# Forming the modulation vectors of a kernel's prologue on two engines, with its panels reordered and late constants

## The reference, cut to what matters

```python
for l in range(DEPTH):
    ada = jax.nn.silu(c) @ w_ada[l] + b_ada[l]                 # c [1, 1024], w_ada[l] [1024, 6144]
    sh_m, sc_m, g_m, sh_f, sc_f, g_f = jnp.split(ada[:, None, :], 6, axis=-1)
    h = rms_norm(x, norm_mix[l]) * (1.0 + sc_m) + sh_m         # x [1, 256, 1024]
    (q_a, kc_a, vc_a, ks_a, ...) = jnp.split(h @ w_in[l], split_at, axis=-1)
    ...
```

## Time and profile before

| | us |
|---|---|
| median of 3 runs | 2214.38 (2214.07 to 2215.04) |
| the profiled execution | 2202.08 |
| its span | 2200.3 |
| TensorE busy in the span | 2052.1 (93%) |
| VectorE busy | 1482.0 (67%) |
| ScalarE busy | 1096.7 (50%) |
| GpSimd busy | 25.0 (1%) |

### The profile page before, as it was taken

The page is one execution under the profiler, slowest core; times in us unless marked ns, Lnnn a source line. Parts: engine busy times, 40 slices in busy tenths (PEclk is TensorE's granted clock), DMA queues, the critical chain, the costliest instruction groups (busy, mean ns, idle before and its releaser), DMA issues. The chain is left out here.

```text
span 2200.3 us, 32166 instructions
## 1 busy us (share of the span) xinstructions
PE 2052.1 (93%) x12896; PEld 1830.2 (83%) x12896; DVE 1482.0 (67%) x2412; ACT 1096.7 (50%) x1738; POOL 25.0 (1%) x46
## 2 busy tenths in 40 slices
PE   3899899999899899999998889899999997889999
PEld 2779888888789888898896668788898897788888
DVE  6677678877685586567757475577667757645774
ACT  2545445544545355445545554455455545545552
POOL 0101000000000000000000000000000000000000
PEclk7999999999999999999999989999999998799999
DMA  8535448876354376556555224256555553232554
GB/s 296 161 134 200 171 135 280 269 266 197 133 192 142 127 225 197 182 182 189 178 189 173 96 77 134 89 179 191 178 182 181 178 166 115 77 115 91 181 184 139
DMA packets 266068, 372.42 MB, mean 169 GB/s; under 512 B 8384, under 2 KB 160192, under 8 KB 265920
## 3 DMA queue, kind: packets, MB, share of 16 engines
q1 hardware_dynamic: 264224, 367.48, 51.4%
q10 hardware_dynamic: 1696, 2.89, 0.4%
HBM read 369.28 MB, written 1.05 MB: 168 GB/s over the span
## 5 line engine op out<-in xcount | busy, mean ns | idle before, releaser
L2081 DVE TENSOR_TENSOR parts<-ring,parts 128x2048 fp32r<-128x2048 f32 (+3 forms) x308 | 680.3, 2210 | 449.8 <-ACT parts L663 449.4
L663 ACT ACTIVATE parts<-ring 128x2048 fp32r<-128x2048 f32 (+3 forms) x308 | 569.5, 1849 | 630.6 <-PE psum L1377 328.5
L1377 PE MATMUL psum<-h,parts 128*128 128x512 f32 x1920 | 676.4, 397 | 0.0
L1375 PE MATMUL psum<-h,parts 128*128 128x256 f32 x1920 | 539.7, 281 | 2.4 <-DVE parts L2081 2.4
L1377 PEld LDWEIGHTS psum<-h,parts 128*128 128x128 f32 x1920 | 360.5, 188 | 87.2
L1375 PEld LDWEIGHTS psum<-h,parts 128*128 128x128 f32 x1920 | 362.7, 189 | 3.1 <-DVE parts L2081 3.0
L1369 PE MATMUL psum<-h,parts 128*128 128x256 f32 (+1 forms) x2088 | 269.3, 289 | 10.8 <-DVE h L2081 4.7
L1369 PEld LDWEIGHTS psum<-h,parts 128*128 128x128 f32 (+1 forms) x2088 | 259.0, 194 | 13.8 <-issue 12.2
L1369 PE MATMUL psum<-parts,h 128*128 128x512 f32 (+1 forms) x864 | 216.1, 405 | 13.2 <-DVE parts L2081 12.0
L1369 PEld LDWEIGHTS psum<-parts,h 128*128 128x128 f32 x864 | 164.7, 201 | 49.0 <-issue 8.1
L1369 PE MATMUL psum<-hid_hl,parts 128*128 128x256 f32 x1584 | 189.9, 282 | 0.9 <-DVE parts L2081 0.9
(11 more groups left out here) (241 smaller groups left out, 2201.5 us busy)
## 6 DMA issues: line engine op xcount, KB each, us to landing
ring<-in_w_ada SPq DMA_DIRECT2D x48, 1024.0 KB, 5.5
ring<-in_w_ffn_in SPq DMA_DIRECT2D x88, 512.0 KB, 4.9
ring<-in_ffn_w_gate SPq DMA_DIRECT2D x88, 512.0 KB, 4.0
ring<-in_ffn_w_up SPq DMA_DIRECT2D x88, 512.0 KB, 5.0
ring<-in_w_in SPq DMA_DIRECT2D x36, 1024.0 KB, 5.0
ring<-in_ffn_w_down SPq DMA_DIRECT2D x32, 1024.0 KB, 5.1
ring<-in_w_ffn_out SPq DMA_DIRECT2D x16, 1024.0 KB, 5.1
ring<-in_ffn_w_down SPq DMA_DIRECT2D x16, 768.0 KB, 4.4
```

The source lines that it names most:

```text
L663: act.activation(out, in_, func, **kw).then_inc(*sig(name, *keys))
L1375: pe.matmul(bank[:, 0:S], wt_hl[1], act[:, 0, :], start=start, stop=False, skip_group_check=True)
L1377: return pe.matmul(bank.rearrange("p (a s) -> p a s", a=2), wt_hl[0], act, start=False, stop=stop, skip_group_check=True)
L2081: dve.tensor_tensor(out, a, b, op).then_inc(*sig(name, *keys))
```

## The change

1. The order of the first panels. Before: groups 0, 1, 2, 3 (two panels each), then win 1 panel 0, win 1 panel 1. After: group 2, group 0, win 1 panel 0, group 1, group 3, win 1 panel 1.
2. Groups 0 and 1 (shift) are made on TensorE (`row_of`): eight fp32 products with one column of `scol` as the stationary operand and 512 weight columns moving, summed in one PSUM row; ScalarE copies the row to SBUF (`row_copy`); four products with a single 1 turn it into four columns. Group 2 and 3 stay on VectorE.
3. The norm of layer 0 is in two parts: chunks 0 to 3 after groups 2 and 0, chunks 4 to 7 after groups 3 and 1. TensorE runs both rows ahead of the first product, and group 3's column sums after three of its eight chunks.
4. `angles` runs at VectorE's start, sine and table load on ScalarE after the squares of `x`.
5. `cols` is loaded ahead of `x`. Only 416 columns of `const` are loaded at the start; rows, the other constants, `pe` and `w2` are issued by SP behind the last panel of the first product.

```diff
-ADA_FIRST = 4
+ADA_FIRST = (2, 0, 1, 3)
+N_FIRST = 416        # const: ident, ones, tri, inv come first
...
-    for i in range(ADA_FIRST):
-        ada(0, i)
+    for i in ADA_FIRST:
+        for n in range(2):
+            src = rows(w["w_ada"][0])[:, 4 * n:4 * n + 4, 512 * i:512 * i + 512]
+            out.append((("ada", 0, i, n), "first", [(0, src)]))
+    late = out[4:]
+    del out[4:]
     for l in range(L):
         win = w["w_in"][l]
         for i in ORDER:
             group(("win", l), i, win, EDGES[i], EDGES[i + 1])
+            out[-1:-1] = late
+            late = []
...
+        ada_row = {i: tok[0:1, 512 * i:512 * i + 512] for i in range(2)}
...
@@ sync
-            for name, dst, src in (("x", x[:], w["x"].rearrange("(c p) t -> p c t", p=P)),
-                                   ("cols", cols[:], w["cols"])):
+            for name, dst, src in (("cols", cols[:], w["cols"]),
+                                   ("x", x[:], w["x"].rearrange("(c p) t -> p c t", p=P))):
...
+                if key == (("win", 0), ORDER[0], 1):
+                    for name, dst, src in (
+                            ("rows", rowsb[:], w["rows"].broadcast_to([P, N_ROW])),
+                            ("masks", const[:, N_FIRST:N_CONST], w["const"][:, N_FIRST:N_CONST]),
+                            ("pe", pe_t[:], w["pe_t"]), ("w2", w2[:], w["w2"])):
+                        sp.dma_start(dst, src).then_inc(
+                            *sig(f"load_{name}", f"loaded {name}", by=16))
...
@@ scalar
-                    if c == 3 and meanwhile is not None:
+                    if c == (3 if prior else chunks - 1):
                         meanwhile()
...
                 stats(st, x, squares, DC, D, lambda c: x_ready(st, c), prior,
-                      (lambda: splits.until((first, g, 0))) if prior else None)
+                      (lambda: splits.until((first, g, 0))) if prior else trigs)
+                if prior is None:
+                    splits.until((first, g, 0))
+                    row_copy(0)
+                    normed_hi(st, range(4), h, shift)
+                    row_copy(1)
                 splits.until((first, g, 1))
-                normed_hi(st, DC, h, shift)
+                normed_hi(st, range(DC) if prior else range(4, DC), h, shift)
...
+            def trigs():
+                act.wait_ge(*at("angles"))
+                run(trig[:], turn[:, 0:2], ACT.Sin, "act_trig", "trig")
+                act.preload_act_table_set(EXP_LN)
+
+            def row_copy(i):
+                job = ("ada row", 0, i)
+                act.wait_ge(*at(("full", job)))
+                run(ada_row[i], psum[0:1, tally.bank(job), :], ACT.Copy, "act_copied",
+                    ("copied", job), ("free", job))
...
@@ tensor
+            def row_of(i):
+                key = ("ada row", 0, i)
+                b = open_bank(key, (BANKS + i,))
+                for half in range(2):
+                    panel = ("ada", 0, i, half)
+                    v = raw(panel, 4, 512)
+                    pe.wait_ge(*at("silu c"))
+                    pe.wait_ge(*at(("panel", panel)))
+                    for c in range(4):
+                        n = 4 * half + c
+                        mm = pe.matmul(b[0:1, :], scol[:, n:n + 1], v[:, c, :], start=n == 0,
+                                       stop=n == DC - 1)
+                    mm.then_inc(*sig("pe_ada", ("released", panel),
+                                     *([("full", key)] if half else [])))
+                pe.wait_ge(*at(("copied", key)))
+                b = open_bank(("ada", 0, i), (BANKS + i,))
+                for j in range(4):
+                    mm = pe.matmul(b[:, j:j + 1], ada_row[i][:, P * j:P * j + P], ones[0:1, 0:1],
+                                   start=True, stop=True)
+                mm.then_inc(*sig("pe_ada", ("full", ("ada", 0, i))))
...
-                    for i in range(ADA_FIRST):
-                        ada_cols(0, i, (BANKS + i,))
+                    ada_cols(0, 2, (BANKS + 2,))
+                    for i in range(2):
+                        row_of(i)
...
-                whole_of(win(1))
+                steps = win(1)
+                if l == 0:
+                    advance(steps, 3)
+                    ada_cols(0, 3, (BANKS + 3,))
+                whole_of(steps)
...
@@ vector
                 refine(rstd[:], newton[:, 0, :], newton[:, 1, :])
+                if vectors is not None:
+                    vectors(0)
...
                 for c in range(chunks + 1):
+                    apart = vectors is not None and c == 4
                     if c:
                         settle()
+                    if apart:
+                        low(3)
+                        vectors(1)
...
+            angles()
             dve.wait_ge(*at("silu c"))
-            for i in range(ADA_FIRST):
-                ...
+            for n in range(2):
+                ada_add(("ada", 0, 2, n))
...
+                def vectors(n):
+                    first = (("win", 0), ORDER[0], n)
+                    if n:
+                        for half in range(2):
+                            ada_add(("ada", 0, 3, half))
+                        ada_take(0, 1)
+                        ada_take(0, 3)
+                    else:
+                        ada_take(0, 2)
+                        ada_take(0, 0)
+                    adaptive(0, 8, "norm_mix", 4 * n, 4 * n + 4)
+                    splits.until(first)
```

More of the change, by code:

```diff
@@ L161, in wide @@
             group(name, g, a, c, min(c + width, a.shape[1]), deep)
-    def ada(l, i):
-        for n in range(2):
-            out.append((("ada", l, i, n), "ada",
-                        [(0, rows(w["w_ada"][l])[:, 4 * n:4 * n + 4, 512 * i:512 * i + 512])]))
     def between(first, stage, every):
@@ L419, in ada_acc @@
         def ada_acc(l, i):
-            if l == 0 and i < ADA_FIRST:
+            if l == 0 and i in ADA_FIRST:
                 return sq[:, i % 2, :]
@@ L426, in ada_acc @@
             return area[:, 512 * (g % 2):512 * (g % 2) + 512]
+        ada_row = {i: tok[0:1, 512 * i:512 * i + 512] for i in range(2)}
         def ada_before(l, i):
+            if l == 0 and i in ADA_FIRST:
+                return None
             stage, g = next((st, groups.index((l, i))) for st, groups in ADA_GROUPS.items()
@@ L683, in _, with stats @@
             splits = Splits(split)
-            def stats(st, src, dst, chunks, width, ready, prior, meanwhile=None):
+            def stats(st, src, dst, chunks, width, ready, prior, meanwhile):
                 for c in range(chunks):
@@ L700, in normed_hi @@
             def normed_hi(st, chunks, dst, shift):
-                for c in range(chunks):
+                for c in chunks:
                     act.wait_ge(*at(("piece", st, c)))
@@ L2142, in ada_add, with norm @@
                         stt(acc, v[:, k, :], c, acc, ALU.mult, ALU.add, "dve_ada", *keys)
-            splits = Splits(split, ada_add, 2 * ADA_FIRST)
-            def norm(st, chunks, gain, dst, src, shift, first, g=0):
+            splits = Splits(split, ada_add)
+            def norm(st, chunks, gain, dst, src, shift, first, g=0, vectors=None):
                 dve.wait_ge(*at(("ln", st)))
@@ L2155, in norm, with low @@
                 refine(rstd[:], newton[:, 0, :], newton[:, 1, :])
+                if vectors is not None:
+                    vectors(0)
+                def low(i):
+                    keys = [("h", st, i)] + [("h", st, "last")] * (i == chunks - 1)
+                    dve.wait_ge(*at(("h hi", st, i)))
+                    stt(dst[:, 1, i, :], piece[:, i % 4, :], shift(i),
+                        dst[:, 0, i, :].bitcast(F32), ALU.add, ALU.subtract, "dve_normed", *keys)
                 for c in range(chunks + 1):
+                    apart = vectors is not None and c == 4
                     if c:
                         settle()
+                    if apart:
+                        low(3)
+                        vectors(1)
                     if c < chunks:
@@ L2162, in norm @@
                             ALU.mult, "dve_piece", ("piece", st, c))
-                    if c >= 1:
-                        i = c - 1
-                        keys = [("h", st, i)] + [("h", st, "last")] * (i == chunks - 1)
-                        dve.wait_ge(*at(("h hi", st, i)))
-                        stt(dst[:, 1, i, :], piece[:, i % 4, :], shift(i),
-                            dst[:, 0, i, :].bitcast(F32), ALU.add, ALU.subtract, "dve_normed",
-                            *keys)
-                        if i == 2:
-                            splits.until((first, g, 1))
+                    if c >= 1 and not apart:
+                        low(c - 1)
+                    if c == 3 and vectors is None:
+                        splits.until((first, g, 1))
             def ada_take(l, i):
```

54 lines of the change are left out of this document (14 added, 40 removed).

## The result

The changed kernel takes 2201.1 us, median of 6 executions (2195.05 to 2202.8), where the kernel before took 2214.23 beside it (6 executions, 2207.24 to 2215.86): 0.994 of the time, 95% interval 0.9922 to 0.9959, 13.1 us less. The prediction was 2205.0, 9.4 us less. The sign and the chain of the start came out; the size did not, and the median lies just outside the range, on the fast side.

A forecast was written before the change was run, and what follows sets the result against it. TensorE was taken as the bound from 64.9 us on; its second product starting at 55.0, 9.9 us sooner, less 0.5 downstream, gave 9.4 us: 2214.38 - 9.4 = 2205.0 us, range 2202.0 to 2212.5.

The forecast's parts named there:

- Transfers: Program start: fewer bytes ahead of the first panel, 4.2 us less; x at 7.3 us, panels at 10.1, 12.9, 15.7.
- Angles: Program start: VectorE's 3.6 us and ScalarE's 2.9 us go into idle time, cost nothing, and remove the hole.
- An instruction of a row: Shift rows on TensorE: 0.50 us each taken, between 0.43 and 0.59; first four of row 0 at 0.9.
- the 9.9: Restart of TensorE: second large product starts at 55.0 us, not 64.9, so 9.9 us sooner.
- Rival 2: Start: gain handed back through panel slots; one late landing or slow row leaves 4.5 us, both leave nothing; chance 0.20.
- Downstream: From 64.9 us on: TensorE is the bound, so most of the 9.9 us stays; 0.5 us taken off.
- The third rival: Start: clock stays low through both rows, product ends at 71.0, 6 us later than 64.9; 2220.4 us; chance 0.10.
- Rival 1: Start: rows cost little and the chain is shorter; gain 11 to 13 us, 2202.4 us; chance 0.10.
- Rival 4: Start: sine ends after the sums of squares, so 1/rms is late; given no chance.

The follow-up runs named there:

- consts_early: Changed kernel with all constants loaded at the start again, on ScalarE's queue; 7.3 us less than the kernel before (ratio 0.9943 to 0.9975).
- again_after: The changed kernel measured once more, without an edit; 14.7 us less than the kernel before (ratio 0.9904 to 0.9952).
- angles_late: Changed kernel with angles, sine and table load put back behind the first norm; ratio 0.9993 to the kernel before.
- before_gap: Kernel before with 30 zero products in TensorE's wait ahead of layer 0's key transposes, sums started anew, losing part of one; ratio 0.9984.
- delay9: Changed kernel with nine idle VectorE instructions (4.91 us) ahead of chunk 4 of h; 5.1 us less than the kernel before (ratio 0.9965 to 0.9997).
- before_fill: Kernel before with 30 zero products, added to running sums, in TensorE's wait ahead of layer 0's key transposes; 6.8 us less (ratio 0.9955 to 0.9987).
- after_fill: Changed kernel with 30 zero products, added to running sums, ahead of layer 0's key transposes; ratio 0.9959 to the kernel before.
- best_fill: Changed kernel with zero products in two early TensorE waits and ahead of the key transposes, late constants one panel later; 2191.66 us against 2211.47 before.
- late_fill: Changed kernel with late angles and 30 zero products, added to running sums, ahead of layer 0's key transposes; ratio 0.9962 to the kernel before.
- warm_both: Changed kernel with zero products on TensorE ahead of row 0 (14) and chunk 4 (30); 14.0 us less than the kernel before (ratio 0.9910 to 0.9957).

## Where the prediction was right, and the step that failed

**The start, step by step.** Transfers: x landed for squares at 7.15 (7.3 predicted), group 2 from 9.93 to 16 (10.1 to 16.1). Angles: between 5.9 and 9.5 us on VectorE, the sine at 9.62, no stall: free, as taken. An instruction of a row takes 0.43 us at the high clock (7.06 / 16 is 0.44), the lower bound; 0.50 was taken. At the low clock it is 0.85, but for seven or eight instructions and not four: row 0 took 9.95 us (9.6), row 1 7.06 (8.0). The misses nearly cancelled: the first product started at 37.94 (38.1).

The transfers of the changed kernel, as in the earlier trace rows:

```profile
x<-in_x SPq DMA_DIRECT2D x1, 1024.0 KB, 6.0
...
rowsb<-in_rows SPq DMA_DIRECT2D x1, 736.0 KB, 8.8
...
const<-in_const SPq DMA_DIRECT2D x1, 708.0 KB, 10.0
```

x takes 6.0 us instead of 10.8, as most of the constants no longer stand beside it (8.1 with them back, in consts_early); the constants take longer at their new place than at the old one.

**Where it lost 2 us of the 9.9.** The second w_in panel, issued at 36.25, took 7.4 us to land and not 5.0 to 5.5, beside 1.6 MB of late constants: its high half began at 43.66, the low one at 45.68 (44.6 predicted). Then GpSimd, released at 45.51 by the landed rows, works while VectorE makes h: 0.77 us an instruction where the earlier trace rows have 0.48. I had put the tables down as harmless since they are not on the path; they were, beside it. Chunk 4 came at 50.25 (48.4) and TensorE's wait was 4.52 us (2.7). The high half of the next panel, at 52.75, stands right behind chunk 7 of h on ScalarE: 56.97 us and not 55.0. The clock fell once more behind the wait and made the first product some 1 us longer, beside this chain. Rival 2 had named this direction (the slots and the constants slipping a late panel), with a price of 4.5 us; the second panel's high half slipped by 1.7 (42.0 expected). One sum of the prediction is off by 0.5 us: the next panel, with its slot free at 39.4 and 5.0 and 4.5 us to come, would land at 48.9 and not at 49.4. It changed nothing, as the high half was not expected before 50.8; the panel took 10.5 us and landed at 50.4.

**The step that failed: "Downstream".** "What comes after should move with that point", less 0.5 us: the term was -0.5 and measured +5 to +6 (13.1 - 7.8 = 5.3, 14.7 - 8.7 = 6.0). I took the time behind the first products as a fixed length that moves as a block. It is not fixed, because the clock in it is not. I had read the earlier trace rows to 102 us only, where the clock is 0.98 on average, and looked at how busy TensorE was, not at how its waits and the clock behind them would change.

The traces say this only in part. Take the sooner start from each gain of the table; what is left came about behind the start. Of the eighteen traces, the kernel before among them, nine have a clock of 0.96 or more from 65 to 300 us, and in them 5.6 us are left on average (2.7 to 10.4); in the nine with 0.95 or less 1.2 us (-3.8 to 5.8). By the wait alone the parting is poorer: the nine with 2.7 us have -0.2 to 6.1, the other three with 3.8 us -3.8, -2.1 and 3.3.

The mean clock of every execution, which was taken along with its time, says it more fully. One minus this clock, times the span, is what TensorE lost to the low clock in that execution (an upper estimate, as it counts the idle time in these stretches too). From it goes the part that falls ahead of the first low half, by the traces 15.4 us in the kernel before and 3.4 in again_after.

| run | clock, mean of its executions | beside it, before | lost less behind the start, us | gain of the mean beyond the start, us |
|---|---|---|---|---|
| again_after | 0.9648 | 0.9575 | 4.8 | 6.3 |
| angles_late | 0.9610 | 0.9575 | -4.2 | -2.6 |
| before_gap | 0.9595 | 0.9578 | 3.9 | 3.5 |
| delay9 | 0.9609 | 0.9573 | -1.4 | -1.7 |
| before_fill | 0.9603 | 0.9571 | 7.4 | 6.0 |
| after_fill | 0.9629 | 0.9571 | 2.0 | 0.3 |
| best_fill | 0.9663 | 0.9571 | 7.3 | 8.6 |

Worked out for all sixteen repeats and experiments, each with the part ahead of the low half from its own trace, the two last columns differ by 1.8 us at most, and their correlation is 0.93. So what the kernels gain or lose beyond the start is what the clock gives or takes there; for the changed kernel this is some 5 of the 6 us. That the clock can be moved without touching the start, and takes the time along, is shown by before_fill, and less surely by late_fill, whose interval (0.9945 to 0.998) barely meets that of angles_late (0.9976 to 1.0009).

**The third rival.** The rows did bring the clock back to its high level after 6 us and held it through row 1. The Trainium skill, "TensorE: Matmul & The Clock Gate", section "HAM oscillation — how this bites in real kernels", tells of short bursts of thin products between waits that all run at the low clock: the trace bears it out for the first half of row 0, at 0.51, and not for the rest, as row 1 ran at 1.00.

**The other rivals.** Rival 1 (11 to 13 us, 2202.4) has nearly the right time for the wrong reason: its 0.43 us held, its restart at 51.8 did not. Even warm_both, with both rows at the high clock, restarts at 54.16:

```profile
54.16 5.69 PE L1391 MATMUL psum<-parts,h 128*128 128x512 f32 x24 [1.14 <-DVE parts L2134]
```

That the measured median lies 1.3 us from this rival's is luck. Rival 4 fell at once: the sine ended at 9.97, four microseconds ahead of the sums of squares. The chances given to a smaller gain and to rival 3 (0.30 together) went to sizes of the start, and none to a larger effect behind it; that is why the range ended at 2202.0.

**What stays open.** Why the low stretches fall where they do. warm_both has the long wait and a clock of 0.98, delay9 the short one and 0.94, and delays ahead of chunk 4 cost more at the end than they take. These runs show that the placing depends on what stands ahead of it and differs between executions of one kernel; they give no rule by which to forecast it, nor do they say why the changed kernel's clock is the better one. How the whole gain divides among the parts of the change is not shown to the microsecond either, as the intervals of the single kernels overlap.

## What to carry to other kernels

A shift at the start of a long kernel is not passed on one to one when TensorE's clock moves behind it: read the granted clock over the whole stretch that is to be shifted, and give the range a term for it in both directions, here some 5 us. One trace is one execution: compare the mean clocks of all executions, not those of two traces. A wait of TensorE there, filled with products of zeros added to a running sum, is a cheap trial (6.8 us in the kernel before, nothing in the changed one, on intervals of some 4 us to either side). "Late" constants share the queues with the panel that is critical at that moment, and what they release, here GpSimd's tables, runs beside VectorE's critical instructions.

## What was not expected of the hardware

- An fp32 product with one column as the stationary operand and 512 moving columns takes 0.43 us an instruction (two to a product) at the high clock and 0.85 at the low: the columns alone, by the 0.214 us for 256 of the earlier trace rows, and nothing on top.
- VectorE's instruction with two tensors, 128x256, takes 0.48 us alone and 0.67 to 0.77 beside GpSimd's, a low half 2.44 instead of 2.29.
- A 1 MB panel takes 5.0 us from issue to landing, 7.4 to 7.8 with further transfers under way, at 390 GB/s in all, and 10.5 when it is queued behind 1.6 MB of them.
- Keeping TensorE at work through a wait of 3.8 us in the kernel before took 6.8 us off the time (2204.63 against 2211.47, ratio 0.9955 to 0.9987), though nothing in the order of the work became sooner.
- The granted clock from 65 to 300 us is anywhere from 0.93 to 0.98 among kernels whose work in that stretch is the same but for 30 idle products, and it differs between two executions of the changed kernel (0.98 and 0.96). In the executions of one kernel the time follows the mean clock: in the 29 of the kernel before beside again_after, 0.001 of it goes with 1.8 us (correlation -0.82).
